# Expert stage of a two-layer diffusion trunk: second expert matrix as stationary operand in 64-column tiles, sixteen-megabyte weight ring, loads in half-megabyte pieces

## The reference, cut to what matters

```python
aff = softmax(xf @ router); gate, idx = top_k(aff.T, cap)
xe = xf[idx]                                    # 16 experts x 80 tokens x 1024
he = silu(xe @ w1) * (xe @ w3)                  # w1, w3: 1024 x 1024 per expert
ye = (he @ w2) * gate                           # w2: 1024 x 1024 per expert
y  = zeros.at[idx].add(ye)                      # back to the tokens
x  = layernorm(ALPHA * x + g2 * y)
```

## Time and profile before

| | us |
|---|---|
| median of 3 runs (3459.65 to 3464.31) | 3464.21 |
| the profiled execution | 3468.49 |
| span of its trace | 3466.6 |
| TensorE busy in the span | 2812.5 (81%) |
| mean granted TensorE clock | 0.907 |
| bytes moved by DMA | 533.9 MB |

### The profile page before, as it was taken

The page is one execution under the profiler, slowest core; times in us unless marked ns, Lnnn a source line. Parts: engine busy times, 40 slices in busy tenths (PEclk is TensorE's granted clock), DMA queues, the critical chain, the costliest instruction groups (busy, mean ns, idle before and its releaser), DMA issues. The chain is left out here.

```text
span 3466.6 us, 72945 instructions
## 1 busy us (share of the span) xinstructions
PE 2812.5 (81%) x32720; PEld 1898.1 (55%) x32720; DVE 1260.2 (36%) x2711; ACT 519.7 (15%) x1001; POOL 753.1 (22%) x874
## 2 busy tenths in 40 slices
PE   5998884648584999999979988566585859999995
PEld 1555554538534766666425645355474446666662
DVE  1101668774524111111240036786754331111114
ACT  0102331131101000000010022302211100100101
POOL 0000908343220000000010037272430200000102
PEclk9999996869896999999989999878798879999998
DMA  8300000000052988888661000000003259899972
GB/s 349 129 20 36 1 8 4 2 7 3 3 218 104 387 332 333 338 341 345 254 260 62 2 36 1 9 3 7 2 3 113 118 212 359 342 350 349 349 291 79
DMA packets 68854, 533.90 MB, mean 154 GB/s; under 512 B 12704, under 2 KB 14560, under 8 KB 32192
## 3 DMA queue, kind: packets, MB, share of 16 engines
q1 hardware_dynamic: 65472, 518.75, 38.5%
q0 software_dynamic: 3072, 10.49, 1.1%
HBM read 520.43 MB, written 8.78 MB: 153 GB/s over the span
## 5 line engine op out<-in xcount | busy, mean ns | idle before, releaser
L2276 PEld LDWEIGHTS ps<-arena 128*64 128x64 f32 x16384 | 580.7, 138 | 93.2 <-issue 90.6
L2276 PE MATMUL ps<-arena 128*64 128x80 f32 x16384 | 601.5, 235 | 20.5 <-issue 11.7
L2289 PE MATMUL ps<-arena 128*128 128x512 f32 (+1 forms) x1024 | 472.8, 606 | 4.6 <-ACT arena L2339 4.6
L527 PE MATMUL ps<-arena 128*128 128x128 f32 (+1 forms) x1088 | 294.7, 434 | 4.6 <-DVE arena L580 4.6
L2404 DVE TENSOR_TENSOR arena<-arena,ps 128x32 f32<-128x32 f32 (+1 forms) x192 | 45.1, 263 | 686.0 <-ACT arena L2347 686.0
L2289 PEld LDWEIGHTS ps<-arena 128*128 128x128 f32 (+1 forms) x1024 | 165.2, 171 | 221.3 <-issue 210.4
L527 PEld LDWEIGHTS ps<-arena 128*128 128x128 f32 x1088 | 164.3, 191 | 135.1 <-issue 130.1
L2034 POOL DMA_INDIRECT arena<-h_d,arena x32 | 39.3, 1227 | 800.1 <-DVEq L2371 662.8
L2347 ACT ACTIVATE arena<-ps 128x160 f32<-128x160 f32 x128 | 38.9, 304 | 944.0 <-PE ps L2276 944.0
L2384 DVE TENSOR_TENSOR arena<-arena,ps 128x512 f32<-128x512 f32 x140 | 96.2, 687 | 206.1 <-PE ps L2305 158.2
L1982 PE MATMUL ps<-arena 128*128 128x512 f32 x320 | 141.4, 605 | 25.1 <-DMA arena<-in_w_out 25.1
(11 more groups left out here) (347 smaller groups left out, 4152.9 us busy)
## 6 DMA issues: line engine op xcount, KB each, us to landing
arena<-in_ex_w SPq DMA_DIRECT2D x128, 2048.0 KB, 8.7
arena<-in_ex_w SPq DMA_DIRECT2D x128, 1024.0 KB, 7.6
arena<-in_ada_w SPq DMA_DIRECT2D x24, 2048.0 KB, 13.7
arena<-in_w_t SPq DMA_DIRECT2D x34, 512.0 KB, 3.4
arena<-in_w_out SPq DMA_DIRECT2D x4, 2048.0 KB, 10.3
arena<-in_w_tok SPq DMA_DIRECT2D x2, 3712.0 KB, 17.4
h_d<-x_sb SPq DMA_DIRECT2D x10, 512.0 KB, 2.6
arena<-mod_d SPq DMA_DIRECT2D x8, 512.0 KB, 10.8
```

The lines of the kernel that those rows point to most:

```text
L527: i = nc.tensor.matmul(ps[:, n % 8, 0:c1 - c0], ring[:, a % WRING, k, :], e.hT[:, k, c0:c1], start=k == 0, stop=k == KD - 1)
L2276: m = nc.tensor.matmul(gated(j)[c * 64:(c + 1) * 64, f, a, :], w13[:, j, a, k, f * P + c * 64:f * P + (c + 1) * 64], xT[:, x % 2, k, :], s ...
L2289: m = nc.tensor.matmul(ps[0:CAP if x % 2 == 0 else P, 4 + h, :], rows[x % 2][:, f, :], w2[:, (f // 2 + 2) % 4, f % 2, h * 512:(h + 1) * 51 ...
```

## The change

- The second product has w2 as stationary operand, in tiles of 64 columns, and the 80 hidden rows move; its result is transposed (model width on the partitions). VectorE multiplies it by the modulation gate as it leaves PSUM (`weighed`), a pair of experts is transposed back on TensorE (`turn_pair`), ScalarE copies it (`turned`), and it is scattered as before. The context rows of eight experts are collected and scattered once (`turn_context`, `scatter_context`), not per pair; their indices go through a small DRAM tensor.
- w2's layout in DRAM is by 256 output columns, 8 KB rows.
- The ring holds six quarters of w13 and four of w2, 16 MiB. 10 MiB are asked for in `phase_output`, 6 MiB in `phase_route`.
- Each load is cut: a w13 quarter into four DMAs, a w2 quarter into two, each of 512 KiB with a row of 4 KB per partition.
- The sum goes into `x` itself; `yacc`, the gate rows in SBUF and POOL's multiplications are gone, as are three memsets at the start of the block. All eight blocks of a pair's scatter stand in one place, behind `turn_tokens`.

```diff
+WG, WP = 6, 4
-    sp.dma_start(mem["w13"][:, j].rearrange("p a k n -> p (a k n)"), e.d["ex_w13"][e.l, x, j].rearrange("p a k n -> p (a k n)")
-                 ).then_inc(e.S[f"ld_e{j}"], 16)
+    for a in range(2):
+        for k in range(0, KD, 4):
+            sp.dma_start(mem["w13"][q % WG][:, a, k:k + 4, :].rearrange("p k n -> p (k n)"),
+                         e.d["ex_w13"][e.l, q // 4, q % 4, :, a, k:k + 4, :].rearrange("p k n -> p (k n)")
+                         ).then_inc(e.S[f"ld_e{q % WG}"], 16)
...
 # phase_route, SP
+            load_w13(e, sp, WG - 1, mem)
+            for q in range(WP):
+                load_w2(e, sp, q, mem)
             sp.wait_ge(S["ld_rt"], 48)
+            sp.wait_ge(S["top"], 1)
+            for n, src in enumerate((pf, val)):
+                sp.dma_start(e.ctx_d[n].rearrange("(e r) -> e r", r=CAPP), src[:, CAPS:CAP]).then_inc(S["ctx_out"], 16)
+            sp.wait_ge(S["ctx_out"], 32)
...
 # phase_experts, SP
+            for q in range(QUARTERS):
+                if q + WG < QUARTERS:
+                    sp.wait_ge(S["h_ps"], q + 1)
+                    load_w13(e, sp, q + WG, mem)
+                if q >= WP:
+                    sp.wait_ge(S["pr_ps"], q - WP + 1)
+                    load_w2(e, sp, q, mem)
...
 # TensorE
-                m = nc.tensor.matmul(ps[0:CAP if x % 2 == 0 else P, 4 + h, :], rows[x % 2][:, f, :],
-                                     w2[:, (f // 2 + 2) % 4, f % 2, h * 512:(h + 1) * 512], start=f == 0, stop=f == KD - 1)
+            def project(x, j):
+                q = 4 * x + j
+                pe.wait_ge(S[f"ld_f{q % WP}"], 32 * (l * NE + x + 1))
+                pe.wait_ge(S["he"], 4 * x + 4)
+                if q >= 2:
+                    pe.wait_ge(S["pr_sb"], q - 1)
+                for b in range(2):
+                    for f in range(KD):
+                        for c in range(2):
+                            m = nc.tensor.matmul(product(j)[c * 64:(c + 1) * 64, b, :],
+                                                 w2[:, q % WP, f, b * P + c * 64:b * P + (c + 1) * 64],
+                                                 he[:, x % 2, f, :], start=f == 0, stop=f == KD - 1)
+                m.then_inc(S["pr_ps"], 1)
+            def turn_pair(i):
+                pe.wait_ge(S["pr_sb"], 8 * i + 8)
...
+                for b in range(KD):
+                    m = nc.tensor.transpose(ps[:, 6 + b // 4, (b % 4) * P:(b % 4 + 1) * P], yS[:, b, :], e.ident[:, :])
...
                 for j in range(4):
                     gate(x, j)
+                    if j == 0 and x % 2 and i >= 0:
+                        turn_pair(i)
+                        if i == HALF - 1:
+                            turn_context(0)
                     if x:
-                        for n in range(4 * j, 4 * j + 4):
-                            project(x - 1, n)
+                        project(x - 1, j)
+                    if j == 1:
+                        if x + 1 < NE:
+                            turn_tokens(x + 1)
+                        if x % 2 and i >= 0:
+                            scatter(i)
...
 # VectorE
+            def weighed(x, j):
+                dve.wait_ge(S["pr_ps"], 4 * x + j + 1)
...
+                for c0, c1, g in ORDER:
+                    m = nc.vector.tensor_tensor(to, product(j)[:, :, c0:c1], row, ALU.mult)
+                m.then_inc(S["pr_sb"], 1)
```

More of the change, by code:

```diff
@@ L379, in modulation_memory @@
 def modulation_memory(e):
-    first = ARENA - 12 * 2048
-    slots = [e.part(at, KD, 512)[0] for at in
-             (first + 12288, first + 16384, first + 20480, first + 4096, first)]
+    slots = [e.part(gate_place(FREED_GATES + n), KD, 512)[0] for n in range(RING)]
     brow, z = e.part(7424, 6, 512)
@@ L386, in modulation_memory @@
     mt, z = e.part(z, P, rows=96)
-    assert z <= first
+    assert z <= gate_place(WG - 1)
     return slots, brow, mrow, mt
@@ L2017, in expert_memory @@
     r["kept"] = z
-    for n in ("iP", "gP", "iC", "gC"):
-        r[n], z = e.part(z, NE // 2)
+    for n, w in (("iP", NE // 2), ("gP", NE // 2), ("iC", 2), ("gC", 2)):
+        r[n], z = e.part(z, w)
     r["iu"], z = e.part(z, NE, rows=CAP, dt=U32)
     r["iota"], z = e.part(z, NTOK)
[L2022 to L2028, removed]
+    first = ARENA - WG * 4096 - WP * 2048
+    assert z <= first, z
+    r["early"] = gate_place(0)
+    r["w2"] = e.part(first, WP, KD, 256)[0]
+    r["w13"] = [e.part(gate_place(q), 2, KD, 256)[0] for q in range(WG)]
     return r
@@ new lines, in scatter @@
+            def scatter(i):
+                pe.wait_ge(S["g_sb"], i + 1)
+                pe.wait_ge(S["yt_sb"], 2 * i + 2)
+                for k, (t, h) in enumerate(blocks):
+                    n = sample_blocks(i) + k
+                    if n >= 2:
+                        pe.wait_ge(S["sc_ev"], n - 1)
+                    nc.tensor.matmul(ps[:, 6 + h, :], GP[:, (t - 1) * P:t * P], yP[:, h * 512:(h + 1) * 512],
+                                     start=True, stop=True).then_inc(S["sp_ps"], 1)
@@ L2311, in _, with scatter_context @@
+            def scatter_context(g):
+                pe.wait_ge(S["gc_sb"], g + 1)
+                pe.wait_ge(S["yx_sb"], g + 1)
+                for h in range(2):
+                    pe.wait_ge(S["sc_ev"], context_blocks(g) + h - 1)
+                    nc.tensor.matmul(ps[:, 6 + h, :], GC, yC[:, h * 512:(h + 1) * 512],
+                                     start=True, stop=True).then_inc(S["sp_ps"], 1)
             turn_tokens(0)
             for x in range(NE):
+                i = x // 2 - 1
@@ L2420, in _ @@
-            e.done("dve", v)
+            for j in range(4):
+                weighed(NE - 1, j)
+            add_pair(NI - 1)
+            add_context(1)
 NORM2_SEMS = MODULATION_SEMS + (
```

281 lines of the change are left out of this document (134 added, 147 removed).

## The result

The changed kernel takes 3505.9 us (median of 4, 3500.7 to 3508.6) against 3463.7: ratio 1.0114, 95% interval [1.0103, 1.0126]. It is slower by 1.1%, well clear of the noise; the forecast was 3313.

What follows compares the result with a forecast made beforehand. It took TensorE to bound the kernel, DMA close behind. 3468.5 us less 185 of TensorE work plus 34 of DMA waits gave 3317; the median lies 4.3 lower, so 3313, range 3270 to 3400.

Steps and rivals of the forecast that it cites:

- the part on instructions: Expert block: a 16 KB instruction transfer per 128 matmul records takes 4.7 us beside 4 KB rows, up to 10 us per layer.
- rival 3: Expert block: instruction transfers bound TensorE, 6.6 us each, +186 us per layer, 3651 us in all; chance 5%.
- TensorE alone: Stretch from a block's first gate's end to its last gate's end: 502.5 us of TensorE work without waits.
- Scatter run: Eight scatter blocks per pair of experts in one run behind the token turn: 8.6 us against 8.97, no net change.
- Turn: Turning a pair's result back on TensorE, eight transposes of 128 columns: 0.9 us, +6.3 over seven pairs.
- Context: The context's turn and two scatter blocks, once in the stretch: +2.8 us.
- Tail: From the last gate to the norm's first instruction: 25.2 us instead of 40.2, -15.0 in each layer.
- Block start: Start of an expert block: transposed first tokens no longer wait for VectorE's last memset, -2.0 us per layer.
- First loads: Six w13 and four w2 quarters in SBUF at block start, asked for while DMA is little used: no cost.
- the indices' way through DRAM: End of routing, beside POOL's first two gathers: taken as 0 us, bounds 0 and 3.4.
- DMA: Loads in the stretch: 189.1 MB at 370 GB/s take 511 us, 17 us of waits per layer, +34 in all.
- Clock: TensorE's granted clock in the expert block stays at 1.00.

Runs made afterwards that it cites:

- a_big_pieces: Changed kernel with each w13 quarter loaded in one 2 MiB DMA and each w2 quarter in one of 1 MiB, not half-megabyte pieces: 3454.0 us.
- b_pieces: Kernel before the change with each expert load cut into half-megabyte DMAs with 4 KB rows, nothing else: 3471.6 us, ratio 1.0013.
- a_wide_both: Changed kernel with both products (gate and second product) on 128 stationary columns in place of tiles of 64: 3992.8 us, ratio 1.152.

## Why the prediction was wrong

**The failed step** is the part on instructions: "I take the excess of 3.9 us to be waiting behind rows of 16 KB, a quarter of it with 4 KB: 4.7 us". The mechanism, the unit of 128 records and its weight (94 transfers per layer, one wanted each 4.59 us) were right; the division by four was a guess about the queue, with no row behind it. In the count of rival 3, which keeps the scatter and turns apart (78.2 us), a transfer took (610.8 - 78.2) / 92.4 = 5.8 us, and 5.9 in layer 1. Rival 3 said that it decides from 5.6 us. It had 5%, and it is what happened, only lighter than its 6.6 us: +31 and +43.5 per layer against before in place of +111 (688 against 577). The runs and traces give the sizes: the packet of a transfer takes 1.0 us with either row and without loads, and the time before it starts is 4.0 us beside 4 KB rows and 3.8 beside 16 KB ones; without loads no excess, half the bytes 39 us per layer, all of them 117 and 126, and smaller DMAs with smaller rows made it worse by 26 per layer, not better.

I gave 3.75 us with idle DMA and 7.6 with loads, both ends from rows, and then placed the new kernel at 4.7, next to the idle end, by a rule about packets of descriptors and not by a row. The Trainium skill ("DMA: Bandwidth & Descriptors", section "Queues, rings and completion order") has an engine leave a queue after a packet of 9 to 17 descriptors; if that set the wait it would be shorter with 4 KB rows. a_big_pieces disagrees: 43.9 us idle of 300 with the long rows, 48.7 with the short. A page that I had not weighed, "Runtime: NRT & Kernel Launch", section "Instruction fetch mechanics", names the unit (refills of 16 KiB blocks, 256 instructions) and calls the cost of a boundary mostly hidden. The unit agrees with 128 matmuls and their loads; "mostly hidden" holds without loads, where none of the 4.9 idle us of 300 is on issue, and not with them (43.8 of the 48.7).

**What held or missed, step by step.**

- *TensorE alone*: 502.5 forecast, 493.5 measured without loads. A gate and a product quarter take 6.64 us, not 6.89. Product quarters of 64 records in 2.2 us: right.
- *Scatter run* 8.6: 8.96 (1466.62 to 1475.58). *Turn* 0.9: 0.93. *Context* 2.8: 0.97 + 1.88. Right in their price, but a run of 9 us with almost no instructions was taken as neutral. In the changed kernel it is not: 54 us in all.
- *Tail* 25.2: 26.8 and 29.8, with stops on issue of 1.9 and 2.7 us in it. *Block start* -2.0: tokens' turn to first gate 5.70 before, 3.60 after. *First loads* and the indices' way through DRAM: no cost, as said.
- *DMA*: the 17 us per layer of waits for weights did not come; all stops but VectorE's come at the boundaries of transfers. Whether 4 KB rows give 370 GB/s through a block was never tested, since TensorE did not ask for it; the share of 0.95 for 340 GB/s in b_pieces speaks for some 358 at share 1 (an estimate).
- *Clock* 1.00 forecast: 0.99 and 0.96, a term that the sum did not have.
- *Slips of the working* that change nothing: 164 GB/s gives 1153 us per layer, not over 1200; DMA at 350 GB/s gives 3372, not 3365; the gates and products add up to 424.9 us, not 424.3.

## What to carry to other kernels

Count instructions as a resource: matmul records per microsecond, against what their transfers give while loads flow, here 128 per 5.8 to 6.6 us. An edit that makes matmuls shorter and more numerous wins here only down to that pace; look in the trace for stops on "issue" a fixed number of records apart before believing TensorE's own time, and look whether a stop stands inside a group of matmuls or before its first one, where "issue" can also be a wait for weights. Then keep loads in large DMAs with large rows (52 to 59 us here), and place slow work with few instructions between dense parts and not in one run (54 to 61 us). Where a cost has a row at either end, the row nearest to the new condition is the estimate, and no rule moves it without a run.

## What the runs showed of the hardware that was not expected

- 128 matmul records with their weight loads need one 16 KB transfer, which keeps up with 4.4 us when DMA is idle and stops TensorE in more than half of the cases (57 of 95) when it runs at share 0.86.
- The transfer's own packet takes 1.0 us with and without loads; beside loads it starts 4.0 us after the restart, and TensorE goes on 1.4 us after its end.
- In a run of 16 slow matmuls the instruction queue pauses for 7 to 14 us: little is fetched ahead.
- Half-megabyte DMAs with 4 KB rows hold DMA at share 0.95 for 340 GB/s, where 2 MiB and 1 MiB ones with rows of 16 and 8 KB need 0.89 for 342.
- 32-bit matmuls with 128 stationary and 80 moving columns take 116 ns per record, with 64 stationary 35: doubling the tile does not halve the time of the same work but makes it 1.6 to 1.7 times as long (a gate 7.1 us for 4.4, a product quarter 3.7 for 2.2).
- The granted clock was at half behind stops of 2.4 and 3.0 us, and in a_wide_both it was 0.50 over 100 us with TensorE busy throughout.
